# A two-layer block with delta rule and experts on one core: delta-rule steps in two groups of workspaces, ordered by a table of ticks, and the first norm moved ahead of the small vectors

## The reference, cut to what matters

```
decay = _masked_exp(gcum[..., :, None] - gcum[..., None, :], incl)
a = jnp.where(strict, jnp.einsum('nbhik,nbhjk->nbhij', kb, k) * decay, 0.0)
rhs = jnp.concatenate([v * beta[..., None], kb * jnp.exp(gcum)[..., None]], axis=-1)
sol = lax.linalg.triangular_solve(a, rhs, left_side=True, lower=True, unit_diagonal=True)
u, w = sol[..., :dv], sol[..., dv:]
def step(s, inp):
    v_new = uc - jnp.einsum('bhck,bhkv->bhcv', wc, s)
    s_new = s * jnp.exp(g_last)[..., None, None] + jnp.einsum(
        'bhck,bhcv->bhkv', kc * jnp.exp(g_last[..., None] - gc)[..., None], v_new)
    o = jnp.einsum('bhck,bhkv->bhcv', qc * jnp.exp(gc)[..., None], s) + jnp.einsum(
        'bhij,bhjv->bhiv', jnp.einsum('bhik,bhjk->bhij', qc, kc) * dc, v_new)
```

## Time and profile before

| | |
|---|---|
| median of 3 runs | 2853.5 us |
| lowest and highest | 2852.21, 2855.32 us |
| the profiled execution, its own time | 2852.58 us |
| its span in the trace | 2850.8 us |
| busy in the span: TensorE | 2497.5 us (88%) |
| VectorE | 630.4 us (22%) |
| ScalarE | 369.2 us (13%) |
| GpSimd | 151.4 us (5%) |

### The profile page before, as it was taken

The page is one execution under the profiler, slowest core; times in us unless marked ns, Lnnn a source line. Parts: engine busy times, 40 slices in busy tenths (PEclk is TensorE's granted clock), DMA queues, the critical chain, the costliest instruction groups (busy, mean ns, idle before and its releaser), DMA issues.

```text
span 2850.8 us, 52823 instructions
## 1 busy us (share of the span) xinstructions
PE 2497.5 (88%) x24386; PEld 1612.6 (57%) x24386; DVE 630.4 (22%) x1191; ACT 369.2 (13%) x595; POOL 151.4 (5%) x140
## 2 busy tenths in 40 slices
PE   5768997699999999999998967678898959999896
PEld 4536775556656555655656667676467634444343
DVE  1441001300000000000002344551534142222223
ACT  1021001100000000000001221111323011011101
POOL 1000000000000000000000023321201000000000
PEclk9879999799999999999999988888999979999998
DMA  7484333399989989998996200001111249999994
GB/s 280 148 296 147 120 133 126 125 393 353 393 312 352 394 309 393 352 394 315 353 393 228 89 1 1 1 1 60 59 60 59 89 177 399 404 397 398 401 401 186
DMA packets 273245, 676.25 MB, mean 237 GB/s; under 512 B 5876, under 2 KB 9423, under 8 KB 268815
## 3 DMA queue, kind: packets, MB, share of 16 engines
q1 hardware_dynamic: 270608, 666.91, 62.3%
q0 software_dynamic: 2112, 6.04, 0.6%
q10 hardware_dynamic: 318, 0.10, 0.0%
HBM read 671.98 MB, written 1.05 MB: 236 GB/s over the span
## 4 chain that ended last, share of the span: by engine, by line
PE 59%; DMA 10%; DVE 5%; ACT 3%; POOL 3%; issue 2%; SPq 2%; DVEq 0%; POOLq 0%; ACTq 0%
PE ps L691 21%; PE ps L601 14%; PE ps L712 10%; DMA ring<-in_w_exp_up 10%; PE ps L776 5%; ACT arena L1884 2%; SPq L548 2%; PE ps L1075 1%; PE ps L1073 1%; PE ps L1066 1%; PE ps L698 1%; PE ps L674 1%; POOL arena L2236 1%; ACT L1884 1%; POOL arena L2204 1%
## 5 line engine op out<-in xcount | busy, mean ns | idle before, releaser
L691 PE MATMUL ps<-ring,arena 128*32 128x256 f32 x10752 | 598.0, 382 | 16.6 <-issue 15.3
L691 PEld LDWEIGHTS ps<-ring,arena 128*32 128x32 f32 x10752 | 349.0, 111 | 249.6 <-issue 32.0
L601 PE MATMUL ps<-hT,ring 128*128 128x256 f32 (+1 forms) x1792 | 444.2, 409 | 19.6 <-ACT arena L1884 7.3
L1884 ACT ACTIVATE arena<-ps 128x512 f32<-128x512 f32 (+4 forms) x347 | 186.8, 556 | 1960.7 <-PE ps L691 576.1
L601 PEld LDWEIGHTS ps<-hT,ring 128*128 128x128 f32 x1792 | 346.9, 194 | 122.6 <-issue 69.4
L712 PE MATMUL ps<-ring,arena 128*32 128x256 f32 x5376 | 300.5, 379 | 0.0
L776 PE MATMUL ps<-ring,arena 128*64 128x512 f32 x1024 | 233.8, 611 | 29.4 <-DMA ring<-in_w_exp_up 26.5
L712 PEld LDWEIGHTS ps<-ring,arena 128*32 128x32 f32 x5376 | 173.9, 110 | 115.3 <-issue 1.3
L1359 DVE TENSOR_TENSOR arena<-arena,ps 128x384 f32<-128x384 f32 x56 | 31.0, 554 | 825.2 <-ACT arena L1884 825.2
L776 PEld LDWEIGHTS ps<-ring,arena 128*64 128x64 f32 x1024 | 81.1, 141 | 178.9 <-issue 178.9
L601 PE MATMUL ps<-arena 128*128 128x128 f32 (+1 forms) x1144 | 146.1, 290 | 20.6 <-DVE arena L1387 7.5
(11 more groups left out here) (319 smaller groups left out, 1721.5 us busy)
## 6 DMA issues: line engine op xcount, KB each, us to landing
ring<-in_moe_wg SPq DMA_DIRECT2D x56, 2048.0 KB, 11.3
ring<-in_moe_wu SPq DMA_DIRECT2D x56, 2048.0 KB, 16.4
ring<-in_moe_wd SPq DMA_DIRECT2D x56, 2048.0 KB, 17.2
ring<-in_w_exp_gate SPq DMA_DIRECT2D x32, 2048.0 KB, 17.5
ring<-in_w_exp_up SPq DMA_DIRECT2D x32, 2048.0 KB, 18.8
ring<-in_w_exp_down SPq DMA_DIRECT2D x32, 2048.0 KB, 14.8
ring<-in_w_in SPq DMA_DIRECT2D x13, 2048.0 KB, 8.9
ring<-in_w_ada SPq DMA_DIRECT2D x12, 2048.0 KB, 8.1
```

The source lines that it names most:

```text
L601: last = mm(outp, l, r, start=(i == 0), stop=(i == n - 1))
L691: last = mm(flat[32 * q:32 * q + 32, S * r:S * r + S], x_[:, k, 32 * r:32 * r + 32], gu[:, :, k, q * P:(q + 1) * P], start=(k == 0), stop= ...
L1884: return nc.scalar.activation(*a, **k)
```

## The change

**Start.** On each engine the first norm is emitted ahead of the small vectors: ScalarE's squares come right after its loads, TensorE transposes x before the rows, VectorE scales x first and multiplies by the gain as soon as the rows are copied.

**Delta stage.** A step has 12 phases: GRAM 0, INV 1, HALF 2, six levels 3 to 8, KEY 9, VALUE 10, STATE 11. Step s starts at tick 6s, so ticks run from 0 to 29, and in a tick one step has a level while another may have its first or last phases. Each engine walks over the ticks. Even steps work in the arena, odd steps in ring slots 0 to 2 (`work`), and each step and direction has two PSUM banks. For that the loads "hi", "f1", "hz" into these slots now wait for the end of the stage. The semaphores of a level are split by group, and TensorE waits for T and for U apart. A and the decayed key share a tile, so the product k q^T is taken at KEY.

```diff
+        spare = ring[:, 0:3, :].rearrange("p s n -> p (s n)")
+        def work(g, o):
+            return area(8192 + o, H, P) if g == 0 else spare[:, o:o + 512].rearrange("p (a b) -> p a b", a=H)
-        WK = [[area(8192 + 4608 * d + 512 * i, H, P) for i in range(9)] for d in range(2)]
+        WK = [[[work(g, 4608 * d + 512 * i) for i in range(9)] for d in range(2)] for g in range(2)]
...
-        READ = {"k": ("k_proj", 4), "v": ("v2_proj", 4), "q": ("q_proj", 1), "zd": ("zd_proj", 1), "hq": ("hq_proj", 1),
+        READ = {"k": ("S_ready", 8), "v": ("S_ready", 8), "q": ("S_ready", 8), "zd": ("zd_proj", 1), "hq": ("hq_proj", 1),
...
+        FIRST = (0, 6, 12, 18)
+        GRAM, INV, HALF, UPDATE, KEY, VALUE, STATE = 0, 1, 2, 8, 9, 10, 11
+        def in_tick(k):
+            return [(s_, k - FIRST[s_]) for s_ in range(4) if GRAM <= k - FIRST[s_] <= STATE]
+        def levels(k):
+            return [(s_, p - HALF) for s_, p in in_tick(k) if HALF < p <= UPDATE]
...
             pe.wait_ge(*at("table_in", 16))
+            norm_T(0)
             pe.wait_ge(*at("rows_in", 16 * (len(ROWS_A) + len(ROWS_B))))
...
-            norm_T(0)
...
+            def product(s_, d, l):
+                g = s_ % 2
+                Ao, T, (bx, by) = WK[g][d][2 + l % 2], WK[g][d][4], banks(s_, d)
+                pe.wait_ge(*at("Aoff%d_ready" % g, level_count(s_, d, l)))
+                pe.wait_ge(*at("T%d_ready" % g, t_count(s_, d, l - 1)))
+                if l == 1:
+                    pe.wait_ge(*at("U%d_ready" % g, u_count(s_, d, 0)))
+                for h in range(H):
+                    last = mm(bx[:, h, :], Ao[:, h, :], T[:, h, :], start=True, stop=True)
+                last.then_inc(inc("P%d_ready" % g), 1)
+            def step(s_, d, l):
+                g = s_ % 2
+                T, U, P1, (bx, by) = WK[g][d][4], WK[g][d][5], WK[g][d][6], banks(s_, d)
+                pe.wait_ge(*at("P%d_copied" % g, level_count(s_, d, l)))
+                pe.wait_ge(*at("U%d_ready" % g, u_count(s_, d, l - 1)))
...
+            for k in range(FIRST[3] + STATE + 1):
+                for s_, l in levels(k):
+                    for d in range(2):
+                        product(s_, d, l)
+                for s_, p in in_tick(k):
+                    for d in range(2):
+                        if p == GRAM:
+                            gram(s_, d)
+                        elif p == KEY:
+                            key(s_, d)
+                        elif p == VALUE:
+                            value(s_, d)
+                        elif p == STATE:
+                            state(s_, d)
+                for s_, l in levels(k):
+                    for d in range(2):
+                        step(s_, d, l)
+                for s_, p in in_tick(k):
+                    if p == INV:
+                        for d in range(2):
+                            turn(s_, d)
...
             done(V.memset(epsc, EPS), "eps_ready")
+            norm(0)
             ve.wait_ge(*at("colsT_ready", 1))
...
+            norm_copy(0, colA("ln_mix_even", 0, 8))
 
             ve.wait_ge(*at("lam_in", 64))
...
+            norm(0, res, ("x_in", 16))
             ac.wait_ge(*at("cols_ready", 1))
```

More of the change, by code:

```diff
@@ new lines, in step @@
+            def step(s_, d, l):
[3 more added lines that the diff above has]
+                pe.wait_ge(*at("U%d_ready" % g, u_count(s_, d, l - 1)))
+                if l < len(LEVELS) - 1:
+                    for h in range(H):
+                        mm(bx[:, h, :], U[:, h, :], P1[:, h, :], start=True, stop=True)
+                for h in range(H):
+                    last = mm(by[:, h, :], P1[:, h, :], U[:, h, :], start=True, stop=True)
+                last.then_inc(inc("TU%d_step" % g), 1)
@@ new lines, in state @@
+            def state(s_, d):
+                n, g = 2 * s_ + d, s_ % 2
+                kd, vn, qe_, at_, (bx, by) = WK[g][d][1], WK[g][d][4], WK[g][d][7], WK[g][d][8], banks(s_, d)
+                pe.wait_ge(*at("vn_ready", n + 1))
+                if s_ >= 2:
+                    for h in range(H):
+                        chain(by[:, h, :], [(Sd[d][:, h, :], qe_[:, h, :]), (vn[:, h, :], at_[:, h, :])])
+                for h in range(H):
+                    last = mm(bx[:, h, :], kd[:, h, :], vn[:, h, :], start=True, stop=True)
+                last.then_inc(inc("dS_ready"), 1)
@@ new lines, in state @@
+                    done(V.tensor_tensor(Sd[d], Sd[d], over(egl[g][d], P), ALU.mult))
+                    done(V.tensor_tensor(Sd[d], Sd[d], bx, ALU.add), "S_ready")
+            for k in range(FIRST[3] + STATE + 1):
+                for s_, p in in_tick(k):
+                    for d in range(2):
+                        if p == GRAM:
+                            gram(s_, d)
+                        elif p == INV:
+                            start_T(s_, d)
+                        elif p == HALF:
+                            start_U(s_, d)
+                        elif p == KEY and s_ >= 2:
+                            attend(s_, d)
+                        elif p == VALUE:
+                            value(s_, d)
+                        elif p == STATE:
+                            state(s_, d)
+                for s_, l in levels(k):
+                    for d in range(2):
+                        step(s_, d, l)
@@ new lines, in _ @@
+            for k in range(FIRST[3] + STATE + 1):
+                for s_, l in levels(k):
+                    for d in range(2):
+                        product(s_, d, l)
+                for s_, p in in_tick(k):
+                    for d in range(2):
+                        if p == GRAM:
+                            gram(s_, d)
+                        elif p == INV:
+                            turned(s_, d)
+                        elif p == KEY:
+                            key(s_, d)
```

354 lines of the change are left out of this document (174 added, 180 removed).

## The result

| | before | changed | forecast |
|---|---|---|---|
| median, us | 2853.3 (4 runs, 2852.2 to 2855.3) | 2768.1 (4 runs, 2763.4 to 2771.4) | 2762, range 2749 to 2786 |
| changed / before | | 0.970 (95% interval 0.968 to 0.972) | 0.968 |
| profiled execution, own time | 2852.6 | 2766.3 | 2761.1 |
| delta rule's stage | 292.0 | 212.1 | 208.6 |

A forecast was written before the change was run, and what follows sets the result against it. No one engine bounds the delta stage: TensorE waits about 79 us and runs partly at the low clock. Start 8.1 plus stage 83.4 save 91.5 from 2852.6, giving 2761.1, median 2762; range 2749 to 2786.

The forecast's parts named there:

- Start, 8.1: Program start: first projection 9.4 earlier, less 1.3 for a table load at the first softmax; 8.1 saved, bounds 7.7 to 10.
- the start gives nothing: Rival at the start: x lands later or the first projection waits for its weights; 2770, chance 0.05.
- Head (ticks 0 to 2), 17.1: Delta stage's first ticks, step 0 alone: as before, 1652.14 to 1669.20, 17.1.
- Levels and blocks: Ticks 3 to 26: 182 blocks at 0.893, 162.5; first level's low clock 2.2; 20 level waits 2.0; three seams 9.3.
- Seams, 3.1 each: Where one step ends and the next starts: TensorE waits for VectorE's work at INV and HALF; 3.1 each, three 9.3.
- End, 15.5: Ticks 27 to 29, step 3 alone: 14 blocks, 12.5, and chains of about 3; 15.5 instead of 22.1.
- Stage, 83.4 saved: Whole delta stage: 208.6 against 292.0, 83.4 saved.
- Loads, nothing: Loads "hi", "f1", "hz" moved to the delta stage's end: costed at nothing, with 63 us of cover.
- The rest unchanged to a microsecond or two: Sign: the program outside the start and the delta stage stays unchanged to a microsecond or two.
- the clock keeps dropping at the seams: Rival in the delta stage: the seams' waits still trigger the low clock, up to 22 stays; 2784, chance 0.12.
- The stage held by VectorE and GpSimd: Rival in the delta stage: VectorE with GpSimd holds the seams, nine each rather than 3.1; 2780, chance 0.16.

The follow-up runs named there:

- experiment 1: The kernel before with only the start's three moves (norm, norm_T and norm_copy ahead of the rows' transposes): 2850.1, ratio 0.999.
- experiment 9: The kernel before with only the loads "hi", "f1" and "hz" waiting for the end of the delta stage: 2852.8, ratio 1.000.
- experiment 6: Changed kernel, GpSimd's level 2 masks moved a tick later (instruction order unchanged): 2763.5; then VectorE's order at an inverse's start changed, on experiment 8's start: 2763.4.
- experiment 5: The kernel before with GpSimd's scalings of keys and values made during the levels: 2819.0; with T also counted apart from U: 2812.0.
- experiment 3: The kernel before with only T counted apart from U, steps still one after the other: 2843.0, ratio 0.997.
- experiment 8: Changed kernel with TensorE transposing the small vectors' rows first and ScalarE loading the exp table ahead of the softmax: 2756.9, ratio 0.966.

## Why the prediction was right, and where it was off

The forecast, 2762, was 6 below the median of four (4 below that of all nine runs), well inside the range. Against the profiled execution the sum is 5.3 of lead too high, 91.5 for 86.2. By the prediction's steps:

- **Start, 8.1.** The lead after the softmax is 8.0, from a projection at 25.61 (forecast 26.7 to 27.5, 9.4 gained; it was 10.9, since ScalarE's table load, which the sum put behind the landing of x, is done at 7.95 to 9.23, ahead of it) less 1.6 for the low clock in its first 11 us, which the sum did not have, less the table load, which is there as said:
```profile
116.01 1.28 ACT L1956 ACT_TABLE_LOAD   x1 [18.34 <-DVE arena L1535]
```
So two misses of about 1.5 cancel, which was luck. At the stage 7.3 are left. As a gain in the median it is worth 3 alone (experiment 1) and 4.5 to 6.3 on top of the stage (2768.1, or 2766.3 over nine runs, against 2772.7). The rival "the start gives nothing" named a late x; in the one execution of the changed program where the lead was seen to go, the clock between 455 and 545 us took it. That the same happens in the five slower runs of the start alone is likely, not shown.
- **Head (ticks 0 to 2), 17.1:** 17.02.
- **Levels and blocks.** Forecast 162.5 + 2.2 + 2.0 + 9.3 = 176.0, measured 8.41 + 170.73 = 179.1. Of the 3.1 too few, 0.9 lie in the first level: the sum kept only 2.2 over a block count of 5.36, so 7.5, but the level took 8.41 as before (8.42). The other 2.2 are the block itself, the term that was mis-sized. The 176 blocks of the long window keep TensorE busy for 160.37, 0.911 each, where the sum had 0.893 (3.2 more in all), and a bare level starts every 5.58 rather than 5.46. The 0.893 came from four blocks back to back; over whole levels TensorE was busy 22.39 for 24 blocks, 0.933 each. Idle time is 10.4, 0.9 under the sum's 9.3 and 2.0.
- **Seams, 3.1 each:** 2.7, 3.4 and 3.4, with single waits of up to 2.2 where 1 to 1.5 were expected.
- **End, 15.5:** 15.94.
- **Stage, 83.4 saved:** 79.9.
- **Loads, nothing:** nothing (experiment 9).
- **The rest unchanged to a microsecond or two:** not quite, and this is the largest single miss. The lead grows by 2.7 after the stage, 1.7 of it in the first projection, and loses 3.7 in the last expert stage, which takes 484.1 where the kernel before takes 480.4. There TensorE waits for weights, 28.8 where the kernel before waits 26.5:
```profile
PE ps L790 <- DMA ring<-in_w_exp_up: 28.8, 14, 2.6
```
The same is seen with the stage alone (83.6 to 80.0) and with T apart (12.0 to 9.5), and less with the scalings early and T apart (41.1 to 40.2) or not at all (35.1). But it isn't a price of the change: the same program took 480.1 there in the execution of experiment 6, as long as the kernel before. No run shows what decides it.

**The rivals.** That the clock keeps dropping at the seams is wrong for this kernel: 1.00 over 170.7 us with waits of up to 2.2. But it was the right thing to fear. The Trainium skill ("TensorE: Matmul & The Clock Gate", section "A second HAM failure mode: psum-queue depth-cycling") warns of small idle spells; the changed kernel doesn't bear that out. Longer idle times do show a drop behind them: experiment 6's wait of 3.62 (0.53), and the waits of 2.26 and 1.99 with 8 products between them in experiment 5 (0.50). The stage held by VectorE and GpSimd (2780) is wrong in size: the seams wait some 3 each, not nine. The releaser is the one named, VectorE's queue with lines 1738 and 1739 at up to 1.71. GpSimd's part in it is open (experiment 6).

**What the sum did not see.** It counted blocks of products and filled every wait with the overlap, so it had nearly the right total and credited it to the overlap: right in size, and in part for the wrong reason. By the runs, of the 79.9 saved in the stage:

| part | us | from |
|---|---|---|
| scalings made during the levels | 31.7 | experiment 5 |
| T counted apart | 9.9 | experiments 3 and 5 (41.6 together) |
| other operands and order, steps still one after the other | 9.9 | 51.5 - 41.6 |
| overlap of the steps | 28.4 | 79.9 - 51.5 |

The parts are what each adds in this order. An overlap with the scalings still late was not run, and such an overlap may hide some of their waits. A reader of the waits of before could have seen the first part: 20.0 us of TensorE waiting for operations of 1.04 that need no result of the last level, only a free tile. How the 9.9 of the third line divide was not tried.

## What to carry to other kernels

Before overlapping two chains, price each wait of the single chain by its releaser: two fifths of the stage's gain (31.7 of 79.9) was one engine doing independent work too late, and took a few lines. Price such a wait with the clock that falls behind it (here 31.7 for 20.0 of waits). Before reading an experiment on the order of work, look whether the edit changes that engine's list at all. And judge a microsecond gained far ahead of the end by the median of many runs, and by how far it can be followed in the trace.

## What the hardware showed that I had not expected

- A VectorE operation of 128x512 floats from two SBUF tiles takes 0.69 alone and 1.63 to 1.75 beside GpSimd's masks, for several in a row; one that reads PSUM stays at 0.68 beside the same masks.
- Waits of TensorE can cost more than their length: taking away 20.0 us of them, two of 1.07 to 3.48 close together in each step, made the same products 12.3 faster over four steps, 1.2 in the first (behind 2.26 and 1.99) and 4.3 in the last (behind 3.48 and 2.29). Taking away 12.9 us in 20 waits of 0.65, one a level, made no product faster (experiment 3).
- The same 64 products, behind the same waits, took 17.2 us in one execution and 11.5 in another of the same program, and the granted clock was 0.70 and 0.50 against 1.00 and 0.84.
- The granted clock of a trace can read 1.00 where products run slow: in experiment 8, 40 products took the 10.9 us in which 51 fit in another execution of the same program. The count of products tells more than the clock's figure there.
- Nine runs of the changed program spread over 8.2 us (2763.1 to 2771.4), ten of the start alone over 12.8, ten of experiment 8's over 3.7, four of the stage alone over 0.5, and 43 of the kernel before over 6.4. The traces don't show what makes an execution go the one way or the other.
